# Heads of an attention stage in loops, and a row of maxima that goes through DRAM

## The reference, cut to what matters

```python
u = rms_norm(h, norm_mix_g)
z = u @ w_in
...
o_a = bidirectional_attention(q_a, k_a, v_a, GQA_HEAD_DIM ** -0.5)
...
o_b = bidirectional_attention(q_full, k_full, v_b, MLA_QK_DIM ** -0.5)
o = jnp.concatenate([rms_norm(o_a, gqa_out_norm_g), rms_norm(o_b, mla_out_norm_g)], axis=-1)
h = h + o @ w_out
h = h + hierarchical_moe(rms_norm(h, norm_ffn_g), ...)
```

## Time and profile before

| | |
|---|---|
| time of three runs, median (lowest, highest) | 4046.6 us (4045.93, 4051.12) |
| the profiled execution: time, span of the core | 4051.12 us, 4049.3 us |
| mean granted TensorE clock | 0.957 of full speed |
| attention stage, from first scores to the last | about 585 to 2783 us of the span |
| instructions in the trace | 53075 |

### The profile page before, as it was taken

The page is one execution under the profiler, slowest core; times in us unless marked ns, Lnnn a source line. Parts: engine busy times, 40 slices in busy tenths (PEclk is TensorE's granted clock), DMA queues, the critical chain, the costliest instruction groups (busy, mean ns, idle before and its releaser), DMA issues. The chain is left out here.

```text
span 4049.3 us, 53075 instructions
## 1 busy us (share of the span) xinstructions
PE 3724.0 (92%) x16747; PEld 2721.7 (67%) x16748; DVE 2759.5 (68%) x4431; ACT 2378.7 (59%) x4129; POOL 558.6 (14%) x553
## 2 busy tenths in 40 slices
PE   7999948999999999999999999998999479999992
PEld 7888825666666666677767677766888446666661
DVE  5666547888888898878777777854444556666564
ACT  4343303777777777766766767677333045555554
POOL 0000000111111111111110111100000023343330
PEclk9999967999999999999999999999999789999996
DMA  4464662221222212220221122002343068888877
GB/s 168 152 215 161 205 171 78 62 43 25 62 62 62 44 32 54 62 60 7 62 61 41 26 62 50 17 7 70 140 145 125 33 205 240 255 242 235 238 229 275
DMA packets 307899, 453.81 MB, mean 112 GB/s; under 512 B 118198, under 2 KB 245458, under 8 KB 296818
## 3 DMA queue, kind: packets, MB, share of 16 engines
q1 hardware_dynamic: 241766, 359.65, 30.0%
q0 software_dynamic: 18576, 67.64, 7.2%
q10 hardware_dynamic: 47376, 24.26, 2.1%
HBM read 305.48 MB, written 145.85 MB: 111 GB/s over the span
## 5 line engine op out<-in xcount | busy, mean ns | idle before, releaser
L941 ACT ACTIVATE b_p_hi<-b_psS 128x512 fp32r<-128x512 f32 (+1 forms) x1376 | 822.2, 598 | 540.0 <-PE b_psS L1072 531.0
L1072 PE MATMUL b_psS<-b_q,b_k 96*128 96x512 f32 (+3 forms) x3440 | 1047.2, 402 | 4.9 <-DMA b_q<-b_nmxT 2.7
L989 DVE TENSOR_TENSOR b_p_lo<-b_prob,b_p_hi 128x512 fp32r<-128x512 f32 x1152 | 824.9, 717 | 245.0 <-ACT b_prob L944 219.0
L944 ACT ACTIVATE b_prob<-b_psS 128x512 f32<-128x512 f32 (+1 forms) x1376 | 815.2, 592 | 1.1
L1072 PEld LDWEIGHTS b_psS<-b_q,b_k 96*128 96x128 f32 (+3 forms) x3440 | 627.1, 185 | 233.4 <-ACT b_prob L944 7.9
L997 DVE TENSOR_REDUCE b_mx_s<-b_psM 128x1 f32<-128x512 f32 x1024 | 690.1, 686 | 76.3 <-PE b_psM L1103 63.6
L1103 PE MATMUL b_psM<-b_k,b_q 128*128 128x512 f32 (+1 forms) x1280 | 511.7, 421 | 49.6 <-DMA b_v<-V 39.5
L1095 PE MATMUL b_psO<-b_p_hi,b_v_hi 128*65 128x512 f32 x1280 | 514.2, 402 | 16.7 <-DVE b_p_lo L989 15.2
L1095 PE MATMUL b_psO<-b_p_lo,b_v_hi 128*65 128x512 f32 x1280 | 507.6, 397 | 0.0
L1095 PE MATMUL b_psO<-b_p_hi,b_v_lo 128*65 128x512 f32 x1280 | 507.4, 396 | 0.0
L930 POOL TENSOR_TENSOR b_p_lo<-b_prob,b_p_hi 128x512 fp32r<-128x512 f32 x128 | 165.2, 1290 | 1662.4 <-ACT b_prob L944 1662.4
(11 more groups left out here) (247 smaller groups left out, 5228.4 us busy)
## 6 DMA issues: line engine op xcount, KB each, us to landing
e_w_gu<-w_gate SPq DMA_DIRECT2D x32, 1024.0 KB, 7.6
e_w_gu<-w_up SPq DMA_DIRECT2D x32, 1024.0 KB, 9.8
e_w_dn<-w_down SPq DMA_DIRECT2D x32, 1024.0 KB, 13.5
a_x_raw<-xallT SPq DMA_DIRECT2D x25, 512.0 KB, 4.9
a_x<-xall SPq DMA_DIRECT2D x25, 512.0 KB, 4.2
c_o<-O SPq DMA_DIRECT2D x24, 512.0 KB, 4.9
c_x<-xall SPq DMA_DIRECT2D x24, 512.0 KB, 3.3
H<-c_h SPq DMA_DIRECT2D x24, 512.0 KB, 2.6
```

The source lines that it names most:

```text
L941: nc.scalar.activation(p_hi[0:kn, (s * NI + j) % NP, :], psS[0:kn, j % 2, :], ACT.Exp)
L944: nc.scalar.activation(prob[0:kn, (s * NI + j) % NP, :], psS[0:kn, j % 2, :], ACT.Exp).then_inc(p_ready, 1)
L989: nc.vector.tensor_tensor(out, prob[0:kn, slot, :], p_hi[0:kn, slot, :].bitcast(F32), ALU.subtract).then_inc(lo_ready, 1)
L1072: m = nc.tensor.matmul(psS[0:kn, j % 2, :], kk[s][0:r, k], qq[s][0:r, q], start=n == 0, stop=n == len(passes) - 1)
```

## The change

`over_heads` becomes two loops of the hardware and two pairs written out. `Fori(a, b)` runs its body for i = a to b-1 on one engine; there are 4 GQA pairs and 4 MLA pairs, so each loop runs three times. Inside, head numbers are register expressions, and so are the values of all waits that depend on them and the DRAM addresses of loads and stores. Each engine runs its own loop.

The row takes another way: SP writes `nmxT` to a DRAM tensor `MX` of 3072 numbers, waits until it is written (`row_kept`), and a second DMA reads `MX` into the partition. DVE waits for the write of the row before, no longer for its landing in `q0` or `q1`.

```diff
-            for i in range(HEADS // 2):
-                lasts = []
-                for h in (2 * i, 2 * i + 1):
-                    lasts.append((h < GH, h + 1 < GH if h + 1 < HEADS else None, h + 1 == HEADS))
-                pair(i, lasts)
+            with engine.Fori(0, GH // 2 - 1) as i:
+                pair(i, [(True, True, False)] * 2)
+            pair(GH // 2 - 1, [(True, True, False), (True, False, False)])
+            with engine.Fori(GH // 2, HEADS // 2 - 1) as i:
+                pair(i, [(False, False, False)] * 2)
+            pair(HEADS // 2 - 1, [(False, False, False), (False, None, True)])
...
                 sp.wait_ge(row_made, n + 1)
+                sp.dma_start(t["MX"].rearrange("(a b) -> a b", b=P), nmxT[:, :].bitcast(F32)).then_inc(row_kept, 16)
+                sp.wait_ge(row_kept, 16 * n + 32)
                 dst = q1[s][GD:GD + 1, :] if gqa else q0[s][QKD:QKD + 1, :]
-                sp.dma_start(dst.bitcast(F32).rearrange("o (a b) -> o a b", b=P), nmxT[:, :].bitcast(F32)).then_inc(row_loaded, 16)
+                sp.dma_start(dst.bitcast(F32), t["MX"].rearrange("(a b) -> a b", a=1)).then_inc(row_loaded, 16)
                 sp.wait_ge(row_loaded, 16 * n + 16)
...
                 dve.wait_ge(t_psum, u + 1)
-                if not isinstance(n, int) or n > 0:
-                    dve.wait_ge(row_loaded, 16 * n)
+                dve.wait_ge(row_kept, 16 * n + 16)
                 nc.vector.tensor_copy(nmxT[:, :], psT[0:TILES, 260:388])
...
             for b in range(2):
                 dve.sem_inc(o_stored[b], 16)
+            dve.sem_inc(row_kept, 16)
```

More of the change, by code:

```diff
@@ L748, in stage_attend @@
         row_made = sem("row_made")
+        row_kept = sem("row_kept")
         row_loaded = sem("row_loaded")
@@ L2241 @@
     "V": ([KEYS, NV * VC], F32),
-    "O": ([TOK, D], F32),
+    "MX": ([TOK], F32), "O": ([TOK, D], F32),
     "H2": ([P + TOK, D], F32), "U2": ([P + TOK, D], F32),
```

## The result

The changed kernel takes 4092.3 us (median of six runs, 4085.8 to 4102.3) against 4047.1 us of the kernel before (six runs, 4044.6 to 4051.1): a ratio of 1.0113, 95% interval 1.0100 to 1.0128. It is slower by 45.2 us. The forecast was 4068 us with a range to 4088: the sign was right, the size a little under half. The profiled execution took 4096.7 us (span 4094.8), 45.5 us over that of before, so the two traces show the whole difference.

A forecast was written before the change was run, and what follows sets the result against it. PE was taken to bound the kernel, DVE close behind. Terms 2.7 + 0.5 (row), 13.2 (branches), 3.4 (clock) and 1.2 (register instructions) sum to 21.0 us; on the 4046.6 us median that gives 4068 us, range 4051 to 4088.

The forecast's parts named there:

- What bounds the kernel: Attention stage: PE, busy 92% of the span, sets the pace, with DVE close behind in a GQA head.
- The row: Row's way through DRAM: second DMA adds 2.7 us at head 0 and 0.5 us at one late row.
- The back-edges: Four taken loop branches, bodies too large to stay: PE stands 3.3 us each for instruction fetch, +13.2 us.
- +3.4 us: Half chance at each of four taken branches that PE's pause drops the clock, costing 1.7 us.
- part 4: DMA addresses from registers, on SP's loads and ACT's output stores: a few tenths per load, costed at nothing.
- their misses (8 KB) run beside PE's: At taken branches, DVE's and ACT's instruction fetches overlap PE's, so only PE's 3.3 us per edge was charged.
- Register instructions: Computed wait values inside the loops: hidden except once a head, 12 x 0.1 = +1.2 us.
- register work reaches PE in every item: Rival: computed waits are exposed in each attention item, 21 + 62 us, 4130 us; chance 0.09.
- The test by the earlier trace: Stage one, loop iteration against straight last round over 40 us: 38.19 against 38.09 us PE busy, no loss showing.
- Cheap edges: Rival: code at taken branches is held or fetched ahead, 0.4 us each, 6.0 us in all, 4053 us; chance 0.17.
- late rows at every head: Rival: the row's second DMA comes late at each of 15 rows, 2 us each, 4098 us; chance 0.03.
- faster: Rival: half-clock stretch at the meta block vanishes in 12 looped heads, 20 us back, 4032 us; chance 0.03.

The follow-up runs named there:

- VectorE's loop alone: Changed kernel with hinted loops on VectorE only, the four other engines' heads written out: 4074.1 us, 1.0068 of the kernel before.
- The row alone: Changed kernel with all 16 heads written out, keeping only the row's new way through DRAM: 4048.5 us, 1.0005 of the kernel before.
- The hint: Changed kernel with its loops asked to hint the back-edge to their engine ahead of the branch: 4068.1 us, 1.0048 of the kernel before.

## Why the prediction was wrong

**What bounds the kernel** was right. TensorE sets the pace, and VectorE is close enough that its delays count: VectorE's loop alone, with branch stops of about 1 us, costs 28 us.

**The row** was put at 2.7 us for head 0 and 0.5 for a late one. PE starts at 657.92 in place of 656.86: 1.1 us. The second leg takes 1.9 us, a short transfer; the piece of 16 KB was the wrong neighbour. The first leg, which I took to cost what the old DMA cost, takes 1.3 us, 1 us less. The row alone measures 1.0005, which allows for anything from 2 us less to 6 us more.

**The back-edges** were the right mechanism. They miss, they stop TensorE for "issue" right after the transposes at four places, and the body's size against the loop of the earlier trace rows is the reason that was given; no run here changes the size by itself. The Trainium skill ("Runtime: NRT & Kernel Launch", section Instruction fetch mechanics) says that a taken branch out of the window stalls until its block is fetched; the trace agrees, with 3.6 to 5.6 us on PE where the untaken branch takes 0.08. The hint, which leaves the branch and takes the stop away, settles it: the stop is not the branch itself.

The step that failed is the size of this term, "I take 4 x 3.3 = +13.2 us" with the clock's "+3.4 us": 16.6 us. It measured 18.3 us of pauses and 12.3 us of lost clock, 30.6, and the hint gives back 26, give or take 9. Two things were left out. First, one unhindered fetch was well judged (3.3 us taken, 3.3 measured with the load moved, 13.1 us in sum), but the second part of the load is issued in those very microseconds, and that is the 5.2 us more of pauses. The prediction had it in the earlier trace rows, where one landing takes 11.4 us, and in the code, where the load waits for the head's last product, and costed part 4 at nothing. Second, the clock was given half a chance of 1.7 us an edge. It fell at all four, for 3 to 13 us: what PE did before it fell was to stand idle for 2 to 5 us; in the hinted kernel, with no such pause, the windows at the first edge are granted 1.00. The step "their misses (8 KB) run beside PE's" held as to time: VectorE's stops can hold the pipeline by themselves (35 us with the three other engines'), but beside TensorE's they add nothing that the ratios show, though VectorE waits twice at the last two edges.

**Register instructions**, "12 x 0.1 = +1.2 us", is the second term that failed. It measured 13 us for 8 heads (no branch taken) and 19 us for 12 (stops removed by the hint). The rival that had it ("register work reaches PE in every item", a chance of 0.09) named VectorE's 1.40 us in an item as its ground. The engine was right, the place was not: not in every item (62 us were its price), but for half of it behind VectorE's drains, and there through one subtraction a head that a delay of 0.15 us pushes behind GpSimd's split of v (2.88 us in place of 0.69). The prediction has neither the drains nor this overlap. The other half stays open. The test by the earlier trace rows was of a loop where VectorE is busy 24.4 of 40 us, and couldn't show either. By the prediction's own sign, heads inside the loops longer than those outside, register work was there to be seen.

**Addresses from registers** at nothing stands: SP's and GpSimd's loops alone measure 1.0001, ScalarE's 1.0002, each good to 4 us.

**Cheap edges, late rows at every head, faster**: none occurred; PE waits for the row once, at head 0. The sum as measured, 1.1 + 30.6 + 13 to 19, is 45 to 51 us, and 45.2 were lost.

## What to carry to other kernels

A loop whose body doesn't fit costs a fetch on each engine at each taken edge. Price it with the DMA traffic of that moment, add the half clock that follows a pause of TensorE, and ask for the hint first: here it cost one instruction a trip and took away 26 of the 46 us. Then look for an engine that is nearly the bound and whose register-valued waits stand behind drains, and look in the timeline at what such a delay pushes together: 0.15 us cost 13.8 us over twelve heads where VectorE and GpSimd then ran at once. Writing out that engine alone (VectorE) and looping the other four with the hint kept the kernel at the time of before, 4050.3 us; none of the versions here is faster than before.

## What the runs showed that I had not expected

- A taken back-edge out of the body took 3.1 to 3.7 us of TensorE's time with idle DMA engines and up to 6.6 us with full ones (the loops with the row's old way); VectorE's, with pieces of half the size, 2.8 to 3.2 and 3.4 to 7.3 us, and with full ones a second stop of 3.9 and 4.4 us at the two MLA edges.
- The hint at the head of the body, some 250 to 290 us ahead of the branch, brings this to 0.4 to 0.8 us on TensorE and about 1 us on VectorE, under the same DMA traffic.
- A pause of TensorE of 3.5 us was enough for the granted clock to fall to 1.2 GHz just after it (0.77 in the 4 us from 924); after the changed kernel's pauses, 3.3 to 5.4 us, it stayed there for 3 to 13 us.
- Moving a load by 16 items (of 126 / 86 = 1.5 us each) off a busy moment made the kernel 82 us slower than the changed one (1.0316 against 1.0113), through an engine (GpSimd) that runs its program in order and had looked idle.
- A subtraction of VectorE that takes 0.69 us takes 2.9 us when it starts 0.08 to 0.10 us behind the start of GpSimd's split of v, and 0.69 when it starts just ahead of it.
